# A two-block transformer in float32 on one Trainium2 core: three orders of work changed, and the mixer's fourth to sixth blocks turned by VectorE and SyncE

## The reference

```python
def causal_depthwise_conv3(u, w):
    s = u.shape[1]
    up = jnp.pad(u, ((0, 0), (CONV_W - 1, 0), (0, 0)))
    return up[:, 0:s] * w[0] + up[:, 1:s + 1] * w[1] + up[:, 2:s + 2] * w[2]

def short_conv_mixer(h, w_in, conv_w, w_out):
    bcx = h @ w_in
    b_gate, c_gate, u = jnp.split(bcx, 3, axis=-1)
    y = b_gate * causal_depthwise_conv3(c_gate * u, conv_w)
    return y @ w_out
...
h = h + rmsnorm(mix, a_post_norm[l])
```

## Time and profile before

| | us |
|---|---|
| three runs | 1030.27, 1031.43, 1032.62 |
| median | 1031.43 |
| the profiled execution | 1030.55 |
| its span in the trace | 1028.7 |
| TensorE matmuls busy | 1019.5 |
| VectorE busy | 684.1 |
| ScalarE busy | 566.6 |
| GpSimd busy | 136.5 |

### The profile page before, as it was taken

How to read it: one execution, slowest core, us unless ns; L and a number is a source line. 1 busy time by engine, 2 the same in 40 slices (tenths; PEclk the granted TensorE clock), 3 DMA queues, 4 the chain that set the end, 5 groups by cost and what they waited for, 6 DMA issues and landing times.

```text
span 1028.7 us, 14332 instructions
## 1 busy us (share of the span) xinstructions
PE 1019.5 (99%) x4783; PEld 838.4 (81%) x4783; DVE 684.1 (67%) x1034; ACT 566.6 (55%) x925; POOL 136.5 (13%) x219
## 2 busy tenths in 40 slices
PE   9999999999999999999999999999999999999997
PEld 6999788888877778888888888888887688888886
DVE  5777766556788985656568565656788685655643
ACT  6665644535567864544546454454676854454542
POOL 1100450000143152000014000000400220000002
PEclk9999999999999999999999999999999999999999
DMA  9565667566643477657576765757643355756651
GB/s 366 182 236 179 200 211 236 186 224 198 213 144 126 146 229 245 218 193 239 181 235 211 234 216 192 240 183 243 205 167 123 97 176 173 239 185 237 191 170 46
DMA packets 104175, 203.56 MB, mean 198 GB/s; under 512 B 52977, under 2 KB 57473, under 8 KB 104129
## 3 DMA queue, kind: packets, MB, share of 16 engines
q1 hardware_dynamic: 101952, 197.44, 58.4%
q0 software_dynamic: 1888, 5.17, 1.7%
q10 hardware_dynamic: 288, 0.37, 0.1%
HBM read 187.20 MB, written 1.05 MB: 183 GB/s over the span
## 4 chain that ended last, share of the span: by engine, by line
PE 94%; DVE 3%; ACT 1%; DMA 1%; POOL 1%; issue 1%; POOLq 0%; SPq 0%; DVEq 0%; ACTq 0%
PE pG L2093 17%; PE pG L2094 17%; PE pG L2097 17%; PE pD L2093 12%; PE pD L2097 11%; PE pD L2094 11%; PE pT L2105 1%; DVE w_low L1689 1%; PE pD L2122 1%; PE pG L2386 1%; PE pG L2105 1%; PE pT L2267 1%; PE pD L2105 1%; DMA raw<-in_stream 1%; PE pD L2405 0%
## 5 line engine op out<-in xcount | busy, mean ns | idle before, releaser
L1689 DVE TENSOR_TENSOR w_low<-raw,w_high 128x1024 fp32r<-128x1024 f32 x340 | 410.5, 1225 | 192.2 <-ACT w_high L1366 182.1
L1366 ACT ACTIVATE w_high<-raw 128x1024 fp32r<-128x1024 f32 x340 | 354.4, 1056 | 203.6 <-PE pG L2097 137.2
L2093 PE MATMUL pG<-w_high,xTh 128*128 128x512 f32 (+1 forms) x824 | 316.7, 384 | 0.0
L2097 PE MATMUL pG<-w_high,xTl 128*128 128x512 f32 (+1 forms) x824 | 314.7, 382 | 0.0
L2094 PE MATMUL pG<-w_low,xTh 128*128 128x512 f32 (+1 forms) x824 | 314.6, 382 | 0.0
L2093 PEld LDWEIGHTS pG<-w_high,xTh 128*128 128x128 f32 x824 | 154.7, 188 | 28.1 <-DVE w_low L1689 0.4
L2097 PEld LDWEIGHTS pG<-w_high,xTl 128*128 128x128 f32 x824 | 154.7, 188 | 27.8
L2094 PEld LDWEIGHTS pG<-w_low,xTh 128*128 128x128 f32 x824 | 154.8, 188 | 27.6
L2093 PE MATMUL pD<-w_high,aTh 128*128 128x512 f32 x372 | 145.6, 391 | 0.6 <-DVE w_low L1689 0.6
L2097 PE MATMUL pD<-w_high,aTl 128*128 128x512 f32 x372 | 144.8, 389 | 0.0
L2094 PE MATMUL pD<-w_low,aTh 128*128 128x512 f32 x372 | 144.7, 389 | 0.0
(11 more groups left out here) (294 smaller groups left out, 894.4 us busy)
## 6 DMA issues: line engine op xcount, KB each, us to landing
raw<-in_stream SPq DMA_DIRECT2D x340, 512.0 KB, 4.5
aF<-aB SPq DMA_DIRECT2D x320, 32.0 KB, 2.7
post<-in_posts POOLq DMA_DIRECT2D x5, 512.0 KB, 4.7
early<-in_stream SPq DMA_DIRECT2D x4, 512.0 KB, 12.7
xF<-hg SPq DMA_DIRECT2D x32, 64.0 KB, 2.5
xF<-hg POOLq DMA_DIRECT2D x32, 64.0 KB, 2.3
first_w<-in_stream SPq DMA_DIRECT2D x3, 512.0 KB, 5.4
h<-in_x SPq DMA_DIRECT2D x2, 512.0 KB, 11.6
```

What stands on the lines that cost most here:

```text
L1366: sc.activation(w_high[:, slot(static):slot(static) + CHUNK], raw_of(static), ACT.Copy).then_inc(w_high_done, 1)
L1689: ve.tensor_tensor(w_low[:, slot(static):slot(static) + CHUNK], raw_of(static), w_high[:, slot(static):slot(static) + CHUNK].bitcast(F32), ...
L2093: pe.matmul(dst, ah, hi, start=start, stop=False)
L2097: return pe.matmul(dst, al, hi, start=False, stop=stop)
```

## The change

Four parts:

1. **Mixer.** `MOVED_BLOCKS` = 3, 4, 5. For these, in both halves, the two transposes on TensorE and the reads of `pT` go. VectorE writes its product into `gate` beside the copied part (in runs of 32 columns), a step `V` transposes `gate` by 32x32 blocks into `aB`, SyncE moves it to `aF` with four transfers, and `T` reads `aF`. The columns of the weights, the rows of the down weights and the taps are reordered on the host to match. `T` and `Y` of half 0 are put behind G and D of half 1, and those of half 1 into the next step, behind G, D and T of half 0. Since TensorE no longer passes through `T` there, G of the next block waits itself for the product that reads its bank.
2. **`reload`.** The load of the post norm is issued behind `tables`.
3. **`walk_opening`** of the second network of the first block (FFN2): the step G(0, 0) stands between the two halves of the join, not behind them.
4. **`walk_attention`.** The low part of the first of three weight chunks goes behind the join, to the other two.

```diff
@@ -145,2 +145,5 @@
 RIGHT_ONLY = []
+MOVED_BLOCKS = [3, 4, 5]
+
+
 SPREADS = [(0, 2), (0, 3), (1, 3), (0, 4), (1, 4), (0, 5), (1, 5), (1, 6)]
@@ -200,3 +203,6 @@
     b = s - 1
+    moves, follower_moves = s in MOVED_BLOCKS, b in MOVED_BLOCKS
     step("G", 0, s, 0)
+    if moves:
+        step("V", 0, s, 0)
     if s == 3:
@@ -204,5 +210,10 @@
     step("D", 0, s - 1, 0)
-    step("T", 0, s, 0)
+    if not moves:
+        step("T", 0, s, 0)
     refill(step, freed, 2 if s < 7 else None)
-    step("Y", 0, s, 0)
+    if b - 1 in MOVED_BLOCKS:
+        step("T", 1, b - 1, 0)
+        step("Y", 1, b - 1, 0)
+    if not moves:
+        step("Y", 0, s, 0)
     freed += [ph.g_chunk(b) + i for i in range(ph.cg)]
@@ -211,2 +222,4 @@
     step("G", 1, b, 0)
+    if follower_moves:
+        step("V", 1, b, 0)
     step("D", 1, b - 1, 0)
@@ -215,3 +228,7 @@
         refill(step, freed, 2)
-        step("T", 1, b, 0)
+        if moves:
+            step("T", 0, s, 0)
+            step("Y", 0, s, 0)
+        if not follower_moves:
+            step("T", 1, b, 0)
         refill(step, freed, 1)
@@ -219,4 +236,6 @@
         refill(step, freed, 1)
-        step("T", 1, b, 0)
-    step("Y", 1, b, 0)
+        if not follower_moves:
+            step("T", 1, b, 0)
+    if not follower_moves:
+        step("Y", 1, b, 0)
 
@@ -351,5 +370,8 @@
             step("low", c)
-    else:
+    elif ph is FFN3:
         walk_join(step, 1, ph.index - 1)
-    step("G", 0, 0, 0)
+    if ph is FFN2:
+        walk_join(step, 1, ph.index - 1, ("G", 0, 0, 0))
+    else:
+        step("G", 0, 0, 0)
     if ph is not FFN4:
@@ -464,3 +486,2 @@
     step("second_low", 0, 0)
-    step("low", behind_join[0])
     step("second", 0, 1)
@@ -469,5 +490,3 @@
     step("second_low", 0, 1)
-    if (1, B_INDEX, 1) in MOVED:
-        step("spread", 1, B_INDEX, 1)
-    for c in behind_join[1:]:
+    for c in behind_join:
         step("low", c)
@@ -1030,3 +1049,17 @@
 
-            return network(ph) * (ph.nb - 1) + b + t + shift * (RING // (ph.cg + ph.kd))
+            if ph.mixer:
+                return MOVED_BLOCKS.index(b) + 1
+            return len(MOVED_BLOCKS) + network(ph) * (ph.nb - 1) + b + t + shift * (RING // (ph.cg + ph.kd))
+
+        def turned_blocks(b):
+
+            return b + 1 - len([x for x in MOVED_BLOCKS if x <= b])
+
+        def gate_parts(t):
+
+            return gate[t][:].rearrange("p (q s j) -> p s q j", q=4, s=2)
+
+        def moved_parts(t):
+
+            return aF[t][:].rearrange("p (a s j) -> p s a j", a=4, s=2)
 
@@ -1268,5 +1301,5 @@
                     pool.wait_ge(h_ready[t], 2 * (k + 1))
-                pool.dma_start(post[:], posts_in[k + 1].partition_broadcast(P)).then_inc(post_loaded, 16)
                 if k == MIX.index:
                     tables()
+                pool.dma_start(post[:], posts_in[k + 1].partition_broadcast(P)).then_inc(post_loaded, 16)
 
@@ -1479,2 +1512,4 @@
                     sc.wait_ge(r_ready[t], ph.index + 1)
+                if ph.mixer and b - 1 in MOVED_BLOCKS:
+                    sc.wait_ge(aB_ready[t], moved_block(ph, t, b - 1, 0))
                 sc.activation(gate[t][:], gate_bank(ph, t, b)[:, 0:256], ACT.Copy if ph.mixer else ACT.Silu,
@@ -1484,3 +1519,6 @@
                 if ph.mixer:
-                    sc.wait_ge(actT_psum[t], b + 1)
+                    if b in MOVED_BLOCKS:
+                        sc.wait_ge(aF_moved[t], moved_block(ph, t, b, 0) * 64)
+                    else:
+                        sc.wait_ge(actT_psum[t], turned_blocks(b))
                     if b < 3 and t == 0:
@@ -1490,3 +1528,7 @@
                         sc.wait_ge(conv_done[1], 3 * (b - 2))
-                    sc.activation(cv[b % 3][:, 2 + P * t:2 + P * (t + 1)], pT[t][:, P:2 * P], ACT.Copy).then_inc(cuT_ready[t], 1)
+                    here = cv[b % 3][:, 2 + P * t:2 + P * (t + 1)]
+                    if b in MOVED_BLOCKS:
+                        sc.activation(here.rearrange("p (a j) -> p a j", a=4), moved_parts(t)[:, 1], ACT.Copy).then_inc(cuT_ready[t], 1)
+                    else:
+                        sc.activation(here, pT[t][:, P:2 * P], ACT.Copy).then_inc(cuT_ready[t], 1)
                     sc.wait_ge(cuT_ready[t], 2 * b + 1)
@@ -1501,3 +1543,3 @@
                     if turned_by_pe(ph, t, b):
-                        sc.wait_ge(actT_psum[t], MIX.nb + network(ph) + 1)
+                        sc.wait_ge(actT_psum[t], MIX.nb - len(MOVED_BLOCKS) + network(ph) + 1)
                     else:
@@ -1843,3 +1885,7 @@
                 ve.wait_ge(gate_ready[t], n)
-                if ph.mixer:
+                if ph.mixer and b in MOVED_BLOCKS:
+                    beside_gate = gate_parts(t)[:, 1]
+                    ve.scalar_tensor_tensor(beside_gate, gate_bank(ph, t, b)[:, 256:384].rearrange("p (q j) -> p q j", q=4), rr[t], beside_gate,
+                                            ALU.mult, ALU.mult).then_inc(act_ready[t], 1)
+                elif ph.mixer:
                     ve.scalar_tensor_tensor(act[t][:, 0:P], gate_bank(ph, t, b)[:, 256:384], rr[t], gate[t][:, P:2 * P],
@@ -1855,3 +1901,3 @@
                 ve.wait_ge(act_ready[t], ph.first_block + b + 1 + shift * (RING // (ph.cg + ph.kd)))
-                ve.transpose(aB[t][:], act[t][:]).then_inc(aB_ready[t], 1)
+                ve.transpose(aB[t][:], (gate if ph.mixer else act)[t][:]).then_inc(aB_ready[t], 1)
 
@@ -1870,3 +1916,7 @@
                     ve.wait_ge(conv_done[t], done + 2)
-                    ve.tensor_tensor(yT[t][:], pT[t][:, 0:P], yT[t][:], ALU.mult).then_inc(conv_done[t], 1)
+                    if b in MOVED_BLOCKS:
+                        y = yT[t][:].rearrange("p (a j) -> p a j", a=4)
+                        ve.tensor_tensor(y, moved_parts(t)[:, 0], y, ALU.mult).then_inc(conv_done[t], 1)
+                    else:
+                        ve.tensor_tensor(yT[t][:], pT[t][:, 0:P], yT[t][:], ALU.mult).then_inc(conv_done[t], 1)
                 else:
@@ -2144,3 +2194,3 @@
                 elsewhere = beside(ph, t, b)
-                if b and not ph.mixer and not elsewhere:
+                if b and not elsewhere and (not ph.mixer or b - 1 in MOVED_BLOCKS):
                     pe.wait_ge(act_ready[t], ph.first_block + b + shift * (RING // (ph.cg + ph.kd)))
@@ -2179,3 +2229,3 @@
                 if ph.mixer:
-                    if b:
+                    if b and b not in MOVED_BLOCKS:
                         turn_gated(t, b, ph)
@@ -2499,2 +2549,8 @@
 
+def mixed(b):
+
+    q = np.arange(P)
+    return 32 * (q % 4) + q // 4 if b in MOVED_BLOCKS else q
+
+
 def weight_chunks(w):
@@ -2517,2 +2573,5 @@
             cols = np.concatenate([m[:, wide * b:wide * (b + 1)] for m in inputs], axis=1)
+            if ph.mixer and b in MOVED_BLOCKS:
+                beside_gate = cols[:, 0:2 * P].reshape(-1, 2, 4, 32).transpose(0, 2, 1, 3).reshape(-1, 2 * P)
+                cols = np.concatenate([beside_gate, cols[:, 2 * P:]], axis=1)
             for i, c in enumerate(sliced(cols, spread=ph.index in BOTH_SPREAD)):
@@ -2521,3 +2580,3 @@
                 q = np.arange(P)
-                rows = P * b + q if ph.mixer else 2 * P * b + 64 * (q % 4) + 32 * k + q // 4
+                rows = P * b + mixed(b) if ph.mixer else 2 * P * b + 64 * (q % 4) + 32 * k + q // 4
                 found[ph.d_chunk(b) + k] = output[rows]
@@ -2586,2 +2645,5 @@
 
+    taps = w["a_conv_w"][0].reshape(3, KT, P)
+    taps = np.stack([taps[:, b, mixed(b)] for b in range(KT)], axis=1)
+
     def by_feature(g):
@@ -2597,3 +2659,3 @@
                                  w["ffn2_norm_2"][0], w["q_norm_2"][0], w["kv_norm_2"][0])]
-        + [w["a_conv_w"][0].reshape(3, KT, P).transpose(2, 1, 0).reshape(P, 24)], axis=1))
+        + [taps.transpose(2, 1, 0).reshape(P, 24)], axis=1))
     row = np.concatenate([w["b_sinks"][0], w["ret_decay_fwd_2"][0], w["ret_decay_bwd_2"][0]])
```

More of the change, by code:

```diff
@@ L351, in walk_opening @@
             step("low", c)
-    else:
-        walk_join(step, 1, ph.index - 1)
-    step("G", 0, 0, 0)
+    elif ph is FFN3:
+        walk_join(step, 1, ph.index - 1)
+    if ph is FFN2:
+        walk_join(step, 1, ph.index - 1, ("G", 0, 0, 0))
+    else:
+        step("G", 0, 0, 0)
     if ph is not FFN4:
```

## The result

The changed kernel takes **1032.61 us** (median of 12 runs, 1032.27 to 1034.77); the kernel before takes 1031.05 beside it (12 runs, 1030.27 to 1032.62). The ratio is 1.0016, with a 95% interval of 1.0008 to 1.0023: slower by 1.6 us, less than the 0.2% that counts as a difference here, and 0.8 us above the forecast. The profiled execution took 1033.39 us (span 1031.6), 0.8 more than its median; why is part of the story.

A forecast was written before the change was run, and what follows sets the result against it. TensorE, busy nearly all the span, was taken as the bound. Mixer +2.0 and orders -0.6, -0.3, -0.7 gave +0.4 us on 1030.55, so 1030.95; with 0.9 for the runs' median, 1031.8 us, range 1028.8 to 1034.0.

The forecast's parts named there:

- The transposes: Mixer: six pairs of TensorE transposes removed at 0.21 us a pair, -1.3 us.
- The five waits in the mixer: TensorE waits: fourth block, second half 0.9 us; seventh, first 0.5; fifth and sixth, second 0.3 each; seventh, second 1.3.
- The post norm's order: First network's opening: moving the 512 KB load behind the angles' table clears TensorE's low-part wait, -0.6 us.
- The attention's order: Attention's join: a low part leaves the place ahead of h's second half, ending TensorE's wait, -0.3 us.
- its chunk is a ring's length away from use: Attention: the low part moved back comes 1.9 us later, but its chunk is not needed soon.
- The second network's order: Second network's opening: the gate's product no longer stands behind the join's second half, -0.7 us.
- What moves back by 0.5 us is the second half of a spread: Second network's opening: only this is delayed; its VectorE reader stands behind three low parts of 1.2 us.
- Rival 1: Mixer: chains quicker than placed, so the waits go as well as the transposes, -2.9 us, 1028.5 us; chance 0.20.
- rival 2: Mixer: transfers collide with table and post norm loads, +2.3 us on the sum, 1034.1 us; chance 0.18.
- the one of over 1 us near 92: Mixer: TensorE's transposes wait for the gate's product, the largest wait in the list after the change.
- the turn of `h`: First network: its first turn of h comes some 2 us later than before.
- the sum of +0.4: Whole kernel: mixer +2.0, orders -0.6, -0.3 and -0.7 us, added to the profiled execution's 1030.55.

The follow-up runs named there:

- mixer_only: The changed kernel's moved blocks alone, with the three orders of before, against the kernel before: ratio 1.0014.
- orders_only: The three orders as changed with no block moved, against the kernel before: -0.86, +0.08 and +0.35 us by places, together -0.4 us.
- lows_cut: The changed kernel with two low parts on VectorE cut from 1024 to 64 columns: -1.46 us at the two places together against the changed kernel.
- mended_all: The changed kernel with seventh block's gates before their splits, two of four moves behind the weight load, old attention and second network orders: median +0.5 us against before.
- post_only: The kernel before with only the post norm's load moved behind the table of angles: median 1.3 us below before's.
- second_low_pool: The changed kernel with one operation of the attention's join moved from VectorE to GpSimd: +0.74 us against the changed kernel.
- transposes_twice: The kernel before with the mixer's six pairs of transposes each issued twice: mixer +1.25 us, 0.77 us given back at the first network's opening.
- moves_around: The changed kernel with two of SyncE's four moves of second-half blocks issued behind the next weight load: the mixer loses 0.33 us less than in the changed kernel.

## Why the prediction was right, and where it was not

The forecast of the median, 1031.8, is 0.8 us low, and the case it described is the one that came: waits in the mixer that cost more than the transposes saved, in a sum close to nothing. By its steps:

- **The transposes: right.** -1.3 forecast, 1.25 measured by doubling them (they were not taken out alone), and the Trainium skill's figure would have been wrong by 2 us.
- **The five waits in the mixer: right in place and nearly in size.** 0.9, 0.5, 0.3, 0.3 and 1.3 forecast, 1.23, 0.44, 0.35, 0.33 and 1.20 measured. The first was mis-sized and its cause half wrong: I gave it to the late load and said that with the shortest load the wait is nothing; the load makes 0.4 of it, and 0.8 stays with the load in time.
- **A term left out.** Three of these waits stand ahead of a down product, whose next matmul then comes 0.1 late: 0.3 us. So the mixer is 3.55 + 0.33 - 1.25 = +2.6, where I had +2.0.
- **The post norm's order: right in the sum, and less its own than I said.** -0.6 forecast, -0.86 at its place in every kernel that has it. But `mixer_only` shows 0.59 of it without the order: a TensorE that comes over 2 us late meets a shorter wait, and in the changed kernel the order adds 0.27.
- **The attention's order, -0.3: wrong** (-0.03 here, +0.08 in `orders_only`). The failed step is "its chunk is a ring's length away from use": TensorE wants that low part at 293.6, 1.2 us after `h` is done.
- **The second network's order, -0.7: wrong** (+0.23, +0.35). The failed step is "What moves back by 0.5 us is the second half of a spread": the low parts move back with it, and TensorE reads one of them 0.9 us after the transposes. I followed the operation that was awaited and did not ask what VectorE has to finish before TensorE's next wait. VectorE was busy but for 0.15 us, and `lows_cut` shows that this is the bound.
- **Rival 1 (no waits) and rival 2 (collision with the tables): did not come.** The fifth block's moves landed 4.8 to 5.6 us after their issue, beside the tables' loads, but were read at 77.39 with the last landed at 76.21. The forecast had allowed 5.3 for the last, which took 5.20. So the sign named for rival 2, moves that land after more than 5 us, was there (three of the four), without its cost; the margin was thin, and in `mended_all`, where the last took 6.6 us, a part of the cost came too (about 0.55 us).
- **Signs.** The waits for `aTh` in the mixer, the one of over 1 us near 92, none at the first network's opening, and the turn of `h` 2.3 us later (100.46 against 98.15) were as said. Two of the three places said to be free of waits were not, and the wait near 92 was not the largest.

The step errors (+0.6 in the mixer, +1.2 in two orders, -0.3 at the first network) make 1.5 us; with them the sum of +0.4 would have been +1.9, and the medians show +1.56. The forecast's median is only 0.8 off because before's runs were also 0.4 faster this time than the 1031.43 it started from; that much is luck. What stays open is whether some third place for the mixer's splits avoids both waits, why the medians of `post_only` gain more than its places, and what makes the third network's weight loads late in some executions.

## What to carry to other kernels

Before you move an operation ahead of others to end a wait, add up all that its engine must finish before the next thing that the waiting engine reads: where that engine has no gap, an order only chooses which wait you see. Two edits that end the same wait give it once. And work that you move back to end a wait now stands ahead of the next thing that is needed: look there before you count the wait as won, and measure at the next join. And a step written later in the program moves nothing on an engine that has no other work in between.

## What the runs showed of the hardware

- A 128x512 subtraction on GpSimd took 4.45 us beside three VectorE subtractions with both inputs in SBUF (`second_low_pool`), and 1.26 to 1.30 us in fourteen other places of the same run; the three took 3.49 together, as they do without it in the kernel after.
- A pair of transposes on TensorE costs 0.21 us between the starts of its neighbours (`transposes_twice`), though each is 0.27 us long in the rows.
- The first matmul of 512 columns behind a wait hands over 0.1 us later than usual (0.31 to 0.34 us to its successor's start against 0.23); one behind transposes did so too, without a wait (293.85 to 294.19 in `lows_cut`).
- With half of a block's four moves issued behind a 512 KB weight load, the last 32 KB move landed 6.6 us after its issue (`mended_all`) and 6.4 us (`moves_around`), where it was 5.2 with all four ahead of the load.
- The four 512 KB weight loads of the third network's opening landed 5.5 to 6.0 us after their issue in one execution and 6.0 to 6.8 us in another of the same program.
